# Spilled expert blocks of 64 rows in two tiles instead of 96 in three, in an encoder-layer kernel

## The chip, the cores and the metric

One core of a Trainium2 chip. The metric is the device time of one execution in microseconds (us); of several runs the median is given. Engines are called PE (matmul), DVE, ACT, POOL (vector, activation and general engine) and SP (which only issues loads and stores here).

## The reference, cut to what matters

One layer of a streaming encoder for 1024 prompt rows and 32 sample rows: two recurrent/attention mixers, cross attention to a memory, and a mixture of experts (MoE) with 32 experts of 1024 x 512. A layer norm follows each. The change touches the MoE alone:

```
lg = xt @ w_group + b_group;  g_sel = argmax(lg)              # one of 4 groups
le = (xt @ w_expert + b_expert).reshape(T, 4, 8)
top_v, top_i = top_k(le[rows, g_sel], 2)                      # two experts of 8 in the group
gate = softmax(top_v) * softmax(lg)[rows, g_sel]
for each row and each of its two experts e:
    h = silu(x @ w_gate[e]) * (x @ w_up[e])
    y[row] += gate * (h @ w_down[e])
x = layer_norm(alpha * x + y)
```

There are 1056 rows, so 2112 pairs of row and expert, 66 for an expert in the mean.

## The kernel before

All work is in float32. Projections, attention and recurrence fill the first 1200 us. Then routing, the expert stage and the last norm follow.

*Routing* (DVE from line 1827 on). Masks of the chosen experts are summed over rows, so that each pair gets its rank within its expert (`RR`) and each expert its count (`cnt`). An expert has one dense block of C = 96 rows. What goes beyond is put into spilled blocks of the same size: `ovn` is the number of them for each expert, `TB_` for each pair the block of its expert that it falls into (0 is the dense one), and `RR` becomes its row in that block. There are `NOVER` = 22 places for spilled blocks and `NB` = 54 blocks in all. PE multiplies one-hot matrices `pick` (rows of a block, written by DVE and POOL) and `place` (blocks, two halves of NB columns: the token and its gate) into `tables` (L838), spreads them over the partitions (L845), and DVE turns them into the gather indices `tok_idx` and the gates (L1896 to L1900). `over3` (L1885) finds for each spilled block its expert; `over_i` has the experts and, as its last entry, the number of spilled blocks in use, `n_over`.

*Dense experts*, 32 in a row, double-buffered: POOL gathers the expert's rows from `x2_dram` in three gathers, one for each tile of 32 rows (L2131); DVE transposes them; PE makes gate and up (L864, 192 matmuls of 32 x 256 columns), ACT and DVE the silu and the transposed h, PE the down product (L873, 96 matmuls), ACT scales by the gate, POOL scatters to `y_dram` (L2121). SP's queue loads three weight matrices of 2 MB an expert, gate and up after the gate/up of the expert two before, down after its down product.

*Spilled blocks* (`spilled` on every engine). They run behind the dense experts, under conditions on `n_over`: two written out, the others in a loop. Their weights go through the same two buffers (`sp` L1140 to L1146; the first two blocks wait for the last dense experts). PE does gate/up tile by tile into a bank of its own for each tile (L920), then down tile by tile as the h of each tile arrives (L932); the silu of a tile runs as soon as its gate/up is there (ACT L1420, DVE L1972 to L1980). ACT evacuates two tiles after the second down tile and the third after the third, stores the block with four DMAs (`store_y`, L1379) and waits for them to land before it goes on. On POOL the blocks are not a loop: `NOVER` conditions stand one after another, each with the gathers of one block (L2150 to L2155).

*The end.* When all is stored, ACT raises `fin_ready` (L1446), POOL gathers for every row its two results from `y_dram` (L2166), PE adds them (L954), and the last norm and the stores follow.

`y_dram` has NB x 96 rows of 4 KB and is filled with zeros early (ACT L1196, one DMA). DVE and ACT wait for that DMA (`zeros_out`, L1524 and L1219) before the first attention scores, as the zeros' place is used there.

Of the kernel before, what the change touches and what calls it, by code (L numbers as in the profile page):

```python
# [8 lines left out]
ALU = mybir.AluOpType  # L9
ACT = mybir.ActivationFunctionType  # L10
# [4 lines left out]
KD = D // P  # L15
SEQ, DEC = 1024, 32
T = SEQ + DEC
NT = (T + P - 1) // P
# [4 lines left out]
G, EG = 4, 8  # L23
NE = G * EG
# [1 line left out]
KE = DE // P  # L26
C = 96
NS = C // 32
NOVER = (2 * T) // C
NB = NE + NOVER  # L30
ALPHA = 2.0 ** 0.25
LN_EPS, RMS_EPS = 1e-5, 1e-6
# [19 lines left out]
def build(nc, io):  # L52
    ctx = ExitStack()
    with ctx:
# [64 lines left out]
        def view(_at, names, **n):  # L119
            size = 1  # L120
            for v in n.values():
                size *= v
            return at(_at, size).rearrange(f"p ({names}) -> p {names}", **n)
# [72 lines left out]
        def route(names, **n):  # L196
            size = 1
            for v in n.values():
                size *= v
            rt[0] += size  # L200
            return view(rt[0] - size, names, **n)
# [17 lines left out]
        assert rt[0] <= R + 23552  # L219
        rt[0] = R + 19968  # L220
        overs = route("i e", i=4, e=NE)
        over3 = route("j e", j=NOVER, e=NE)
        gates = route("n a", n=NB, a=NS)
        tokq = route("n a", n=NB, a=NS)
        none_q = route("n a", n=NB, a=NS)
# [208 lines left out]
        def _(pe):  # L434
# [476 lines left out]
            def spilled(j, b, turn_n):  # L911
                pe.wait_ge(o_xt, j + 1)
                pe.wait_ge(o_w[b], 32 * turn_n + 32)
                if isinstance(j, int):
                    pe.wait_ge(y_ready, NE - 1 + j)
                for a in range(NS):
                    for k in range(KD):
                        for q in range(4):
                            out = psum[32 * q:32 * q + 32, (3 * b + a) * BANK:(3 * b + a) * BANK + 256]
                            last = mm(out.rearrange("p (m n) -> p m n", m=2), xeT[:, b, a, k, :],  # L920
                                      gu[b][:, :, k, q * P:(q + 1) * P], start=(k == 0), stop=(k == KD - 1))
                    last.then_inc(o_gu, 1)
                pe.wait_ge(o_down[b], 16 * turn_n + 16)
                if isinstance(j, int) and j == 0:
                    pe.wait_ge(y_ready, NE)
                else:
                    pe.wait_ge(o_y, j)
                for a in range(NS):
                    pe.wait_ge(o_h, 3 * j + a + 1)
                    for k in range(KE):  # L930
                        for q in range(4):
                            last = mm(O_Y[32 * q:32 * q + 32, a * 256:(a + 1) * 256], hhT[:, b, a, k, :],  # L932
                                      wd[b][:, k, q * 256:(q + 1) * 256], start=(k == 0), stop=(k == KE - 1))
                    if a > 0:
                        last.then_inc(o_dn, 1)

            with pe.If(n_over > 0):
                spilled(0, 0, 0)
# [21 lines left out]
        def _(sp):  # L960
# [173 lines left out]
            def spilled(j, b):  # L1134
                e = sp.value_load(over_i[0:1, bass.ds(j, 1)], min_val=0, max_val=NE - 1)
                if isinstance(j, int):
                    sp.wait_ge(gu_done, NE - 1 + j)
                else:
                    sp.wait_ge(o_gu, 3 * j - 3)
                sp.dma_start(gu[b][:, 0], dyn(gate_w, e)).then_inc(o_w[b], 16)  # L1140
                sp.dma_start(gu[b][:, 1], dyn(up_w, e)).then_inc(o_w[b], 16)
                if isinstance(j, int):
                    sp.wait_ge(y_done, NE - 1 + j)
                else:
                    sp.wait_ge(o_dn, 2 * j - 2)
                sp.dma_start(wd[b], dyn(down_w, e)).then_inc(o_down[b], 16)  # L1146
# [26 lines left out]
        def _(act):  # L1173
# [200 lines left out]
            gate_rows = [psum[:, a * BANK:a * BANK + NS * 256].rearrange("p (s m n) -> p s m n", m=2, n=P)[:, :, 0, :]  # L1374
                         for a in (0, 2)]

            def store_y(rows, slot, s):
                for q in range(4):
                    act.dma_start(rows[:, 256 * q:256 * q + 256].rearrange("(a t) n -> t a n", t=32),  # L1379
                                  ye[slot][32 * q:32 * q + 32]).then_inc(s, 16)  # L1380

            def y_rows(e, b, slot, turn_n):

                act.wait_ge(y_done, e + 1)
# [28 lines left out]
            def spilled(j, b):  # L1413
                if isinstance(j, int) and j == 0:
                    act.wait_ge(h_ready, NE)
                else:
                    act.wait_ge(o_h, 3 * j)
                for a in range(NS):
                    act.wait_ge(o_gu, 3 * j + a + 1)
                    A(sg[:, a, :], psum[:, (3 * b + a) * BANK:(3 * b + a) * BANK + P], ACT.Exp, scale=-1.0)\  # L1420
                        .then_inc(g_exp, 1)
                act.wait_ge(o_gate, j + 1)
                act.wait_ge(o_dn, 2 * j + 1)
                if isinstance(j, int):
                    act.wait_ge(y_out[b], 16 * NS * NE // 4)
                for a in range(2):
                    A(ye[b][:, a, :], O_Y[:, a * 256:(a + 1) * 256], ACT.Copy, scale=gate2[:, b, a:a + 1])
                act.wait_ge(o_dn, 2 * j + 2)
                A(ye[b][:, 2, :], O_Y[:, 512:768], ACT.Copy, scale=gate2[:, b, 2:3]).then_inc(o_y, 1)
                act.wait_ge(o_y, j + 1)  # L1430
                store_y(y_dram[bass.ds(j * C + NE * C, C), :], b, o_out)
                act.wait_ge(o_out, 64 * j + 64)
                A(lnv[:, 0:1], eps_ln, ACT.Copy)

# [27 lines left out]
        def _(dve):  # L1462
# [381 lines left out]
            dve.wait_ge(evac["dve"], jobs[("RK",)][3] + 1)  # L1844
            cnt, ovn, oend, ost = (overs[:, i, :] for i in range(4))

            link(TS(ovn, cnt, 1.0 / C, -(C / 2 + 0.5) / C, ALU.mult, ALU.add))
            link(TS(ovn, ovn, ROUND, -ROUND, ALU.add, ALU.add))
            link(TS(ovn, ovn, 0.0, None, ALU.max))
            link(V.tensor_tensor_scan(oend, one_col.to_broadcast([P, NE]), ovn, 0.0, ALU.mult, ALU.add))  # L1850
# [2 lines left out]
            link(V.tensor_reduce(RR, products, AX.X, ALU.add))  # L1853
            of_chosen(ost, OO)

            link(TS(TB_, RR, 1.0 / C, -(C / 2 - 0.5) / C, ALU.mult, ALU.add))
            link(TS(TB_, TB_, ROUND, -ROUND, ALU.add, ALU.add))
            STT(RR, TB_, -float(C), RR, ALU.mult, ALU.add).then_inc(places_ready, 1)
            link(TS(TA, TB_, 1.0, None, ALU.is_ge))
            link(TT(OO, OO, TB_, ALU.add))  # L1860
            link(STT(OO, OO, float(NE - 1), EE, ALU.add, ALU.subtract))
# [60 lines left out]
            def turn_x(b):  # L1922
                return V.transpose(xeT[:, b], xe[:, b].rearrange("p s (d k) -> p s k d", k=KD))  # L1923
# [32 lines left out]
            n_over = dve.value_load(over_i[0:1, NOVER:NOVER + 1], min_val=0, max_val=NOVER)  # L1956

            def spilled(j, b, turn_n):
                dve.wait_ge(o_x[b], 16 * NS * turn_n + 16 * NS)
                turn_x(b).then_inc(o_xt, 1)  # L1960
                if isinstance(j, int):
                    dve.wait_ge(y_ready, NE - 1 + j)
                    dve.wait_ge(y_done, NE - 1 + j)
                else:
                    dve.wait_ge(o_y, j - 1)
                    dve.wait_ge(o_dn, 2 * j - 2)
                V.tensor_copy(gate2[:, b:b + 1, :], gates[:, bass.ds(j + NE, 1), :]).then_inc(o_gate, 1)
                for a in range(NS):
                    n, s_a = 12 * j + 4 * NE + 4 * a, sg[:, a, :]
                    gate, up = (psum[:, (3 * b + a) * BANK + m * P:(3 * b + a) * BANK + m * P + P] for m in range(2))  # L1970
                    dve.wait_ge(g_exp, 3 * j + NE + a + 1)
                    TS(s_a, s_a, 1.0, None, ALU.add).then_inc(silu_step, 1)  # L1972
                    dve.wait_ge(silu_step, n + 1)
                    V.reciprocal(s_a, s_a).then_inc(silu_step, 1)
                    dve.wait_ge(silu_step, n + 2)
                    TT(s_a, s_a, gate, ALU.mult).then_inc(silu_step, 1)
                    dve.wait_ge(silu_step, n + 3)
                    TT(hh[:, a, :], s_a, up, ALU.mult).then_inc(silu_step, 1)
                    dve.wait_ge(silu_step, n + 4)
                    V.transpose(hhT[:, b, a], hh[:, a, :].rearrange("p (d k) -> p k d", k=KE)).then_inc(o_h, 1)  # L1980
# [42 lines left out]
        def _(pool):  # L2023
# [101 lines left out]

            x2_quarters = x2_dram.rearrange("t (q n) -> (t q) n", q=4)

            def gather(e, b, done):

                for a in range(NS):  # L2130
                    pool.indirect_dma_start(out=xe[:, b, a, :], out_offset=None, in_=x2_quarters,  # L2131
                                            in_offset=bass.IndirectOffsetOnAxis(ap=tok_idx[:, e, a:a + 1], axis=0),
                                            bounds_check=4 * T - 1, oob_is_err=False)\
                        .then_inc(done[a], 16)
# [13 lines left out]
            for j in range(NOVER):  # L2148
                if j == 2:
                    for e in range(NE - 3, NE):  # L2150
                        scatter(e)
                with pool.If(n_over > j):
                    if j < 2:
                        pool.wait_ge(xt_ready, NE - 1 + j)
                    else:  # L2155
                        pool.wait_ge(o_xt, j - 1)
                    gather(NE + j, j % 2, [o_x[j % 2]] * NS)
                if j < 2:
                    scatter(NE - 5 + j)

# [39 lines left out]
```

## Time and profile before

| | us |
|---|---|
| median of three timed runs | 1838.14 (1835.23 to 1840.77) |
| the profiled execution | 1831.85 |
| its span, first to last instruction | 1830.1 |
| PE busy | 1732.0 |
| two spilled blocks on PE | 1742.4 to 1773.5 |

The profile is one execution. Its span is what the engines' instructions cover; the execution's own time has 1.75 us more around it. Times in the rows below are from the span's start. "Busy" of PE is not PE at its peak: matmul ends are modelled. The chain of waits is followed back from the last instruction, at each step to what released it. A row of it gives its start, its length, the engine and line that it lies on, and how many instructions are merged.

### The profile page before, as it was taken

The page shows a single profiled execution, that of the slowest core. Times are in us where ns is not written, and L with a number is a line of the kernel's source. Part 1 is how long each engine was busy: PE and PEld are TensorE (multiplying, and loading weights), DVE is VectorE, ACT ScalarE, POOL GpSimd, SP SyncE. Part 2 cuts the span into 40 slices and gives each one's busy share as a digit, 9 for nine tenths or more (in the row PEclk, how much of TensorE's full clock was granted, in tenths as well). Part 3 has the DMA queues.
Part 4 walks back from the last instruction along what each step waited for, and adds up shares of the span by engine and source line. Part 5 has one row for each costly group of instructions (what it writes and reads, how often), then busy time and mean ns, then how long its engine had stood idle before and what let it go on. Part 6 is the DMA issues. An engine that isn't in the chain of part 4 may idle for free. (4 is left out here: it accounts for less than half of the span.)

```text
span 1830.1 us, 34543 instructions
## 1 busy us (share of the span) xinstructions
PE 1732.0 (95%) x15263; PEld 1085.3 (59%) x15263; DVE 746.0 (41%) x1174; ACT 326.1 (18%) x741; POOL 293.5 (16%) x291
## 2 busy tenths in 40 slices
PE   8999999999999999999998999849999999999976
PEld 4565556645666644445666665536666666666642
DVE  1213456514766753310104333564434443344337
ACT  1212224401334210110002111000111110111116
POOL 2100000001322000000000000043333333333223
PEclk9999999999999999999999999769999999999997
DMA  8951011001002041253100000549999999999957
GB/s 276 310 187 47 1 45 51 1 1 49 1 5 98 5 161 35 73 195 115 46 26 32 24 23 12 192 156 391 420 422 421 422 420 421 422 422 416 391 219 276
DMA packets 66230, 330.70 MB, mean 181 GB/s; under 512 B 14948, under 2 KB 17352, under 8 KB 53088
## 3 DMA queue, kind: packets, MB, share of 16 engines
q1 hardware_dynamic: 47856, 280.70, 38.5%
q0 software_dynamic: 12192, 26.76, 4.0%
q10 hardware_dynamic: 6096, 22.02, 3.9%
q8 instruction: 63, 1.03, 0.2%
q14 instruction: 23, 0.19, 0.0%
HBM read 288.05 MB, written 50.23 MB: 185 GB/s over the span
## 5 line engine op out<-in xcount | busy, mean ns | idle before, releaser
L864 PE MATMUL psum<-arena 128*32 128x256 f32 x6144 | 339.8, 381 | 20.1 <-issue 13.3
L864 PEld LDWEIGHTS psum<-arena 128*32 128x32 f32 x6144 | 230.6, 111 | 127.9 <-issue 33.1
L461 PE MATMUL psum<-arena 128*128 128x512 f32 x640 | 282.2, 600 | 2.9 <-issue 2.9
L1468 DVE COPY arena<-psum 128x512 f32<-128x512 f32 (+6 forms) x128 | 83.8, 663 | 368.0 <-PE psum L461 201.2
L461 PEld LDWEIGHTS psum<-arena 128*128 128x128 f32 x640 | 121.9, 193 | 149.9 <-issue 149.5
L684 PE MATMUL psum<-arena 128*128 128x352 f32 x576 | 177.9, 460 | 0.0
L873 PE MATMUL psum<-arena 128*32 128x256 f32 x3072 | 172.3, 379 | 0.5 <-DVE arena L1920 0.5
L446 PE MATMUL psum<-arena 128*128 128x352 f32 x576 | 170.8, 460 | 0.1
L1178 ACT ACTIVATE arena<-psum 128x128 f32<-128x128 f32 (+7 forms) x193 | 94.1, 497 | 344.8 <-PE psum L439 243.8
L2131 POOL DMA_INDIRECT arena<-x_rows,consts x102 | 103.8, 1017 | 282.8 <-DVE arena L1923 254.0
L873 PEld LDWEIGHTS psum<-arena 128*32 128x32 f32 x3072 | 116.3, 110 | 50.1 <-DVE arena L1920 1.0
L446 PEld LDWEIGHTS psum<-arena 128*128 128x128 f32 x576 | 109.6, 190 | 61.1 <-issue 0.8
L684 PEld LDWEIGHTS psum<-arena 128*128 128x128 f32 x576 | 106.7, 191 | 52.7 <-issue 0.2
L1910 DVE TENSOR_SCALAR arena<-arena 128x384 f32<-128x384 f32 x32 | 11.5, 360 | 298.2 <-ACT arena L1396 298.2
L439 PEld LDWEIGHTS psum<-consts,arena 128*128 128x128 f32 (+4 forms) x783 | 91.0, 153 | 53.8 <-issue 35.3
L439 PE MATMUL psum<-consts,arena 128*128 128x128 f32 (+4 forms) x783 | 113.1, 276 | 10.3 <-POOL consts L2040 4.7
L719 PE MATMUL psum<-arena 128*128 128x512 f32 x256 | 111.3, 593 | 0.0
L2121 POOL DMA_INDIRECT y_blocks<-arena,consts x96 | 96.0, 1000 | 51.2 <-issue 28.4
L1706 DVE SCALAR_TENSOR_TENSOR arena<-arena,psum 128x1024 f32<-128x1024 f32 x16 | 19.5, 1221 | 161.0 <-PE psum L461 88.2
L719 PEld LDWEIGHTS psum<-arena 128*128 128x128 f32 x256 | 48.2, 190 | 57.9 <-issue 57.7
L1912 DVE RECIPROCAL arena<-arena 128x384 f32<-128x384 f32 x32 | 81.7, 2553 | 1.1
L2065 POOL TENSOR_TENSOR arena<-arena 128x1024 f32<-128x1024 f32 x4 | 8.2, 2039 | 432.9 <-DVE arena L1590 432.9
(279 smaller groups left out, 1653.0 us busy)
## 6 DMA issues: line engine op xcount, KB each, us to landing
arena<-in_moe_w_down SPq DMA_DIRECT2D x34, 2048.0 KB, 21.4
arena<-in_moe_w_gate SPq DMA_DIRECT2D x34, 2048.0 KB, 14.5
arena<-in_moe_w_up SPq DMA_DIRECT2D x34, 2048.0 KB, 21.1
y_blocks<-arena ACTq DMA_DIRECT2D x1, 20736.0 KB, 102.2
arena<-in_w_in SPq DMA_DIRECT2D x6, 2048.0 KB, 9.8
arena<-in_x_prompt SPq DMA_DIRECT2D x9, 512.0 KB, 3.3
arena<-in_w_out SPq DMA_DIRECT2D x2, 2048.0 KB, 8.1
arena<-in_xa_wk SPq DMA_DIRECT2D x2, 2048.0 KB, 11.9
```

What stands on the lines that cost most here:

```text
L439: return nc.tensor.transpose(out, a, ident[0:n, 0:n])
L446: last = mm(ps[:, c * BANK:c * BANK + THIRD], lhs(k), rhs[:, k, c * THIRD:(c + 1) * THIRD], start=(k == 0), stop=(k == KD - 1))
L461: last = mm(ps[0:n, c * 512:(c + 1) * 512], lhs(k), rhs(k)[:, c * 512:(c + 1) * 512], start=(k == 0), stop=(k == KD - 1))
L684: last = mm(psum[:, bank * BANK:bank * BANK + THIRD], w_z[name][:, k, m * P:(m + 1) * P], xT[:, k, third(c)], start=(k == 0), stop=(k == K ...
L719: last = mm(psum[0:n, b:b + BANK], mixT[:, k, cols_of(t)], wrows[:, k, c * 512:(c + 1) * 512], start=(k == 4), stop=(k == 3))
L864: last = mm(out, xeT[:, b, a, k, :], gu[b][:, :, k, j * P:(j + 1) * P], start=(k == 0), stop=(k == KD - 1))
L873: last = mm(B_Y[b][32 * j:32 * j + 32, a * 256:(a + 1) * 256], hhT[:, b, a, k, :], wd[b][:, k, j * 256:(j + 1) * 256], start=(k == 0), sto ...
L1178: take(A(out, src, ACT.Copy), key)
L1468: take(V.tensor_copy(out, src), key)
L1912: V.reciprocal(sg, sg).then_inc(silu_step, 1)
L2121: pool.indirect_dma_start(out=y_quarters, out_offset=bass.IndirectOffsetOnAxis(ap=y_idx[:, e, a:a + 1], axis=0), in_=ye[e % 4][:, a, :], i ...
L2131: pool.indirect_dma_start(out=xe[:, b, a, :], out_offset=None, in_=x2_quarters, in_offset=bass.IndirectOffsetOnAxis(ap=tok_idx[:, e, a:a + ...
```

## The change

A spilled block now holds `OVER_ROWS` = 64 rows, in the tiles 1 and 2 of the three; tile 0 of it is left out on every engine. An expert's first 96 rows stay dense; what goes beyond is counted in blocks of 64, and a row's place in its block starts at 32. There are 32 places for spilled blocks instead of 22, and 64 table columns a half instead of 54. `y_dram` grows with NB (each block keeps 96 rows in it). `over3` gets a place of its own in memory. The semaphore counts follow (two a block instead of three).

```diff
-NOVER = (2 * T) // C
+OVER_ROWS = C - 32
+NOVER = 32
 NB = NE + NOVER
@@ pe, spilled
-                for a in range(NS):
+                for a in (1, 2):
                     for k in range(KD):              # gate and up of tile a
...
-                for a in range(NS):
-                    pe.wait_ge(o_h, 3 * j + a + 1)
+                for a in (1, 2):
+                    pe.wait_ge(o_h, 2 * j + a)
...
-                    if a > 0:
-                        last.then_inc(o_dn, 1)
+                    last.then_inc(o_dn, 1)
@@ act, spilled
-                for a in range(2):
-                    A(ye[b][:, a, :], O_Y[:, a * 256:(a + 1) * 256], ACT.Copy, scale=gate2[:, b, a:a + 1])
+                A(ye[b][:, 1, :], O_Y[:, 256:512], ACT.Copy, scale=gate2[:, b, 1:2])
                 act.wait_ge(o_dn, 2 * j + 2)
                 A(ye[b][:, 2, :], O_Y[:, 512:768], ACT.Copy, scale=gate2[:, b, 2:3]).then_inc(o_y, 1)
                 act.wait_ge(o_y, j + 1)
-                store_y(y_dram[bass.ds(j * C + NE * C, C), :], b, o_out)
+                rows = y_dram[bass.ds(j * C + NE * C + 32, OVER_ROWS), :]
+                for q in range(4):
+                    act.dma_start(rows[:, 256 * q:256 * q + 256].rearrange("(a t) n -> t a n", t=32),
+                                  ye[b][32 * q:32 * q + 32, 1:3]).then_inc(o_out, 16)
@@ dve, routing
-            link(TS(ovn, cnt, 1.0 / C, -(C / 2 + 0.5) / C, ALU.mult, ALU.add))
+            link(TS(ovn, cnt, 1.0 / OVER_ROWS, 0.5 - (C + 0.5) / OVER_ROWS, ALU.mult, ALU.add))
...
-            link(TS(TB_, RR, 1.0 / C, -(C / 2 - 0.5) / C, ALU.mult, ALU.add))
+            link(TS(TB_, RR, 32.0, 1.0 / OVER_ROWS, ALU.max, ALU.mult))
+            link(TS(TB_, TB_, 0.5 / OVER_ROWS - 1.0, None, ALU.add))
             link(TS(TB_, TB_, ROUND, -ROUND, ALU.add, ALU.add))
-            STT(RR, TB_, -float(C), RR, ALU.mult, ALU.add).then_inc(places_ready, 1)
+            STT(RR, TB_, -float(OVER_ROWS), RR, ALU.mult, ALU.add).then_inc(places_ready, 1)
@@ dve, spilled
-                dve.wait_ge(o_x[b], 16 * NS * turn_n + 16 * NS)
-                turn_x(b).then_inc(o_xt, 1)
+                dve.wait_ge(o_x[b], 32 * turn_n + 32)
+                V.transpose(xeT[:, b, 1:3], xe[:, b, 1:3].rearrange("p s (d k) -> p s k d", k=KD)).then_inc(o_xt, 1)
...
-                for a in range(NS):
+                for a in (1, 2):                     # silu of tile a
@@ pool
-                    gather(NE + j, j % 2, [o_x[j % 2]] * NS)
+                    gather(NE + j, j % 2, [o_x[j % 2]] * NS, (1, 2))
```

## Rows read from the trace of the kernel before

**Rows 1.** The page: span, and PE's busy time, its share and instructions.
```profile
span 1830.1 us, 34543 instructions
PE 1732.0 (95%) x15263; PEld 1085.3 (59%) x15263; DVE 746.0 (41%) x1174; ACT 326.1 (18%) x741; POOL 293.5 (16%) x291
```

**Rows 2.** The page's DMA issues: what, queue, count, KB each, us to landing.
```profile
arena<-in_moe_w_gate SPq DMA_DIRECT2D x34, 2048.0 KB, 14.5
y_blocks<-arena ACTq DMA_DIRECT2D x1, 20736.0 KB, 102.2
```

**Rows 3.** The chain of waits in the spilled blocks: start, us, what, instructions.
```profile
1742.40 10.36 PE psum L920 x192
1752.76 5.18 PE psum L932 x96
1757.94 10.36 PE psum L920 x192
1768.30 5.22 PE psum L932 x96
```

**Rows 4.** SP's instructions in order of time: start, us, queue, line, what.
```profile
1736.58 0.33 SPq L1146 DMA_DIRECT2D arena<-in_moe_w_down  x1
...
1738.19 0.48 SPq L1141 DMA_DIRECT2D arena<-in_moe_w_up  x1
1742.46 0.33 SPq L1146 DMA_DIRECT2D arena<-in_moe_w_down  x1
```

**Rows 5.** DMA issues of 1736.5-1736.7, 1738.0-1738.3 and 1742.3-1742.6, last column us to landing.
```profile
arena<-in_moe_w_down SPq DMA_DIRECT2D x1, 2048.0 KB, 10.7
...
arena<-in_moe_w_up SPq DMA_DIRECT2D x1, 2048.0 KB, 19.3
...
arena<-in_moe_w_down SPq DMA_DIRECT2D x1, 2048.0 KB, 20.0
```

**Rows 6.** Busy by stretch: us, PE, PEld, DVE, ACT, POOL, granted clock, DMA share, GB/s.
```profile
1736.00:1759.00 23.00, 22.51 (x420) 13.41 (x415) 10.99 (x22) 4.55 (x12) 5.90 (x6) 1.00 1.00 403
```

**Rows 7.** DVE in order of time: the last transpose of block 1's third tile.
```profile
1770.60 0.42 DVE L1980 STREAM_TRANSPOSE arena<-arena 128x128 f32<-128x128 f32 x1
```

**Rows 8.** Busy by stretch as in rows 6, around two pauses of PE before the routing.
```profile
1143.00:1144.00 1.00, 0.00 (x0) 0.00 (x0) 1.00 (x2) 0.12 (x1) 0.00 (x0) 1.00 0.14 53
...
1146.00:1147.00 1.00, 1.00 (x7) 0.93 (x7) 0.90 (x5) 0.00 (x0) 0.00 (x0) 0.50 0.85 328
...
1183.00:1184.00 1.00, 0.62 (x3) 0.62 (x4) 0.96 (x2) 0.33 (x1) 0.00 (x0) 0.58 1.03 442
```

**Rows 9.** The chain of waits: gate/up of the first two dense experts.
```profile
1223.40 22.94 PE psum L864 x384
```

**Rows 10.** DVE in order of time, in the routing: start, us, line, operation, shapes.
```profile
1205.62 0.18 DVE L1857 TENSOR_SCALAR arena<-arena 128x18 f32<-128x18 f32 x1
...
1207.13 0.61 DVE L1875 TENSOR_TENSOR arena<-arena 128x432 f32<-128x432 f32 x1
...
1213.59 0.89 DVE L1885 TENSOR_TENSOR arena<-arena 128x704 f32<-128x704 f32 x1
```

**Rows 11.** In order of time: the zero store's issue, and the first attention steps.
```profile
36.38 0.39 ACTq L1196 DMA_DIRECT2D y_blocks<-arena  x1
...
154.14 0.30 DVE L1532 TENSOR_TENSOR psum<-psum,consts 128x128 f32<-128x128 f32 x1 [0.74 <-PE psum L564]
...
154.89 0.37 ACT L1238 ACTIVATE arena<-psum,consts 128x128 f32<-128x128 f32 x1 [7.15 <-DVE consts L1533]
...
159.45 0.27 PE L439 MATMUL psum<-consts,arena 128*128 128x128 f32 x1
```

**Rows 12.** In order of time: ACT behind block 1, POOL's next step; idle before in brackets.
```profile
1779.02 0.20 ACT L1433 ACTIVATE consts<-consts 128x1 f32<-128x1 f32 x1 [5.00 <-DMA y_blocks<-arena]
1779.34 0.20 ACT L1446 ACTIVATE consts<-consts 128x1 f32<-128x1 f32 x1
1779.82 0.90 POOL L2166 DMA_INDIRECT arena<-y_blocks,consts  x1 [31.79 <-ACT consts L1446]
```

More of the change, by code:

```diff
@@ L221, in build @@
         overs = route("i e", i=4, e=NE)
-        over3 = route("j e", j=NOVER, e=NE)
+        over3 = view(R + 21504 + 2 * NT * G, "j e", j=NOVER, e=NE)
         gates = route("n a", n=NB, a=NS)
@@ L1138, in spilled @@
                 else:
-                    sp.wait_ge(o_gu, 3 * j - 3)
+                    sp.wait_ge(o_gu, 2 * j - 2)
                 sp.dma_start(gu[b][:, 0], dyn(gate_w, e)).then_inc(o_w[b], 16)
@@ L1375, in _ @@
                          for a in (0, 2)]
[L1377 to L1380, printed above, removed]
             def y_rows(e, b, slot, turn_n):
@@ L1416, in spilled @@
                 else:
-                    act.wait_ge(o_h, 3 * j)
-                for a in range(NS):
-                    act.wait_ge(o_gu, 3 * j + a + 1)
+                    act.wait_ge(o_h, 2 * j)
+                for a in (1, 2):
+                    act.wait_ge(o_gu, 2 * j + a)
                     A(sg[:, a, :], psum[:, (3 * b + a) * BANK:(3 * b + a) * BANK + P], ACT.Exp, scale=-1.0)\
@@ L1967, in spilled @@
                 V.tensor_copy(gate2[:, b:b + 1, :], gates[:, bass.ds(j + NE, 1), :]).then_inc(o_gate, 1)
-                for a in range(NS):
-                    n, s_a = 12 * j + 4 * NE + 4 * a, sg[:, a, :]
+                for a in (1, 2):
+                    n, s_a = 8 * j + 4 * NE + 4 * (a - 1), sg[:, a, :]
                     gate, up = (psum[:, (3 * b + a) * BANK + m * P:(3 * b + a) * BANK + m * P + P] for m in range(2))
-                    dve.wait_ge(g_exp, 3 * j + NE + a + 1)
+                    dve.wait_ge(g_exp, 2 * j + NE + a)
                     TS(s_a, s_a, 1.0, None, ALU.add).then_inc(silu_step, 1)
@@ L2126, in _, with gather @@
             x2_quarters = x2_dram.rearrange("t (q n) -> (t q) n", q=4)
-            def gather(e, b, done):
-                for a in range(NS):
+            def gather(e, b, done, tiles=range(NS)):
+                for a in tiles:
                     pool.indirect_dma_start(out=xe[:, b, a, :], out_offset=None, in_=x2_quarters,
```

## The prediction

> **What bounds the kernel now.** I read the page first (span, engine shares), then the chain of waits from its end backwards, then around the two spilled blocks the issues of the load queue with their landing times, the busy times by stretch, and last the engines' order of time in the routing. TensorE (PE) is busy for 95% of 1830.1 us [rows 1], so work taken from it counts, if nothing else is late there. 34 gate loads are issued [rows 2]: 32 experts and two spilled blocks. The chain shows these two at the end of the MoE stage, all on PE and without a gap: gate/up of block 0 from 1742.40, down from 1752.76, gate/up of block 1 from 1757.94, down from 1768.30 to 1773.52 [rows 3]. Each gate/up is 10.36 us for three tiles (3.45 a tile), each down 5.18 (1.73 a tile). The reader should see that "on PE" isn't "because of PE" there: the DMA engines are at a share of 1.00 from 1736 to 1759 at 403 GB/s [rows 6], and the up weights of block 1, issued at 1738.19, take 19.3 us [rows 4, 5], so they land at 1757.5, 0.45 us before PE takes them up.
>
> **How many blocks.** The reference's routing of these inputs gives two experts more than 96 rows: 158 and 105; the next has 94. Over 96 they have 62 and 9 rows, so both forms need one block each: two before, two after.
>
> **The change, part by part** (times on the clock of before). *Block 0.* One tile less: 3.45 + 1.73 = 5.18 us of PE. But the third tile was also a cover. From the end of a gate/up tile to its turned h there are 2.72 us (1768.30 [rows 3] to 1770.60 + 0.42 [rows 7]), for exp, four DVE steps and a transpose. With three tiles PE had two tiles of down (3.46) to do meanwhile; with two it has one (1.73) and waits about 1.05 with the hand-over. So gate/up ends at 1749.3, h of the last tile at 1752.0, down at 1753.8: 4.1 us earlier than 1757.94. Its down weights are there (1736.58 + 10.7 = 1747.3 [rows 4, 5]).
> *Block 1.* Its up weights land at 1757.5 as before: the load's issue waits for the last dense experts, not for block 0, and the queue ahead of it is the same. Block 0's store now goes out at about 1754.4 and shares the DMA engines with that load: 0.26 MB at 403 GB/s [rows 6] is 0.6 us at most; I take half. So block 1 starts at about 1757.9, where it started before, and block 0's 4.1 us are lost in a wait for weights. What remains is block 1's own saving, the same 4.1 us. Its down weights (1742.46 + 20.0 = 1762.5 [rows 4, 5]) are still ahead of their use at 1764.8.
> *The clock.* PE, so far without a pause, now stands for 1.05 us and then for 4.1 us. The trace has like pauses: it was idle through 1143 to 1144 at clock 1.00, and at 1146 to 1147, busy again, it had 0.50; after a pause to 1183.4 the clock is 0.58 in 1183 to 1184 [rows 8]. That is the fall from 2.4 to 1.2 GHz. Its price stands in the chain: two gate/up of 192 matmuls after a pause took 22.94 us [rows 9] where two at full clock take 20.72 [rows 3], so 2.2 us. Bounds: 0 (no fall) and 6.9 (all of block 1's gate/up at half speed). I take 2.2. The Trainium skill speaks against the change at this place: "TensorE: Matmul & The Clock Gate", section "HAM oscillation — how this bites in real kernels", says that a burst of matmuls shorter than the wait for its next transfer lets the clock drop, so that the next burst starts at half rate. By that rule the sum below is as it stands; without it it would be 2.2 us lower; the trace agrees in its pauses before the routing and shows nothing of it among the experts, where no such pause exists.
> *The last store and what follows.* PE's end to ACT's next step is 5.5 us (1773.52 [rows 3] to 1779.02 [rows 12]): evacuation, four issues, landing. A third fewer bytes: between 0 and 1.8 (a third of 5.5); I take 0.5, as issue and latency stay. The gather of the pairs and the last norm shift as a whole.
> *Routing.* Here nothing but routing runs, and DVE is its chain, so every step counts. One more scalar step: 0.2 [rows 10]. The tables get 64 columns a half for 54. An operation on 432 elements takes 0.61 us and one on 704 takes 0.89 [rows 10], 1.03 ns an element. Six large place operations of 80 more elements: 0.5. The block-to-expert compare and its sum, 704 to 1024 elements: 2 x 0.33 = 0.66. The transposes' PE work and four reads of the tables: some 0.25. Sum 1.6, at 1.2 to 2.0; PE's own table matmuls grow beside it and end first. The first weight loads of the expert stage wait for the first expert, so the whole stage moves by 1.6.
> *Zero fill.* y_dram grows from 54 to 64 x 96 rows. The store, issued at 36.38 [rows 11], lands after 102.2 us [rows 2], at 138.6; in proportion to its bytes it would take 121 and land at 157.5. DVE's first step that waits for it ran at 154.14, the exponential after it at 154.89 for 0.37, and PE wants its result no earlier than 159.45 [rows 11]; so the fill may land up to 158.3 and cost nothing. I take 0; what if it is later stands below.
> *POOL.* Ten more skipped conditions; 6 gathers of the blocks become 4. POOL waits 31.79 us after its last scatter [rows 12], with 20 such conditions in that time, so 30 are hidden at any price below 0.98 us. ACT passes a skipped condition and four waits in 0.12 us (1779.22 to 1779.34 [rows 12]). I take 0. The smaller transposes, the dropped copy on ACT and the other index offsets lie beside PE or loads: 0.
>
> **Sum.** +1.6 (routing) − 4.1 (block 1) + 2.2 (clock) − 0.5 (store) = −0.8. The span goes from 1830.1 to 1829.3, that execution from 1831.85 to 1831.0. It was quicker than all three timed runs (1835.23 to 1840.77); I take the difference over to their median: 1838.14 − 0.8 = 1837.3. The bounds of the terms alone give −4.7 to +4.8.
>
> **Rivals.** *The clock holds.* For: the fall comes late, not yet at 1143 to 1144, and could fall behind block 1's gate/up. Against: both pauses of [rows 8] were followed by it. −3.0: 1835.1.
> *The weights come in time*, because a freer DMA queue brings block 1's up weights by 1753.8. For: only 0.45 us show that they are late at all. Against: the share of 1.00 [rows 6]. Both blocks save 4.1 without a fall: 1.6 − 8.2 − 0.5 = −7.1: 1831.0.
> *The zero fill is late.* It decides from 158.3 on. If the next 2 MB weight load (L1002, after the queries' projection) falls into its end and is served first, the fill loses 5.2 us more (2.1 MB at 403 GB/s [rows 6]) and lands at 162.7: 4.4 us on the first attention scores: 1841.7. Against: that load is one of two that take turns.
> *POOL's conditions set the end* (the other side). At the bound, 31.79 / 20 = 1.59 us each, 30 take 47.7 and the pair gathers begin at 1797.3 instead of 1778.9, so +17.6: 1855.7. It decides from 0.98 us on. Against: ACT's 0.12.
> *The change doesn't keep the count*: an expert with more than 160 rows needs two blocks of 64. The largest has 158, two rows of room. A third block's loads queue behind the others: its up weights would land 2 x 5.1 us (2.1 MB at 403 GB/s) after 1762.5, at 1772.7; PE then ends at 1784, 10.6 later than before, with clock and routing +13: 1851.
>
> **How the numbers follow.** Forecast 0.60; the clock holds 0.18; weights in time 0.08; zero fill late 0.05; POOL 0.04; a third block 0.03; something else 0.02. A measurement of this kernel tells about 0.3% (5.5 us) from no change. Below 1832.6 lie the weights in time and a little scatter of the two likeliest: 0.12. Above 1843.7 lie POOL, the third block, the worst of the zero fill and scatter: 0.10. Between: 0.78. The range takes in the weights in time and most of the late fill and leaves out POOL and the third block: 1831 to 1842.5.
>
> **What would show it.** In the profile of after: gate/up of the blocks with 128 matmuls each and down with 64; a PE pause of about 4 us ended by a DMA before block 1, whose up weights land near 1757.5 + 1.6; a granted clock of 0.5 in part of block 1's gate/up; one wait of about 1 us within each down; the first expert 1.6 us later; two blocks (34 gate loads); the zero store landing before PE's first wait in attention. If block 1 starts 4 us earlier, or the clock stays, the tail steps are wrong; if the first expert isn't later, the routing step is; if POOL's pair gathers begin after ACT's last step by more than 0.5 us, POOL's is.

## The result, and the profile after

| | before | after |
|---|---|---|
| time, median of 20 runs each | 1837.65 us (1831.43 to 1847.25) | 1842.4 us (1836.69 to 1853.84) |
| ratio | | 1.0036, 95% interval 1.0019 to 1.0052 |
| profiled execution, its span | 1831.85, 1830.1 us | 1842.33, 1840.6 us |
| granted clock, mean | 0.976 | 0.971 |

In the text, before and after name the two kernels. The change makes the kernel a little slower: 4.75 us between the medians, where 0.8 us less was forecast. The time lies within the range given; the sign is that of the rival "the zero fill is late". Executions of one kernel lie up to 17 us apart; in every profile but that of before PE runs a part of attention (mostly within 217 to 250 us) at half clock, and the longer this stretch, the longer the execution (6 to 7 us of it in h2's, which took 1833.55 us, some 30 in f2's of 1848.05); so the kernels are compared by medians and intervals, and the profiles stretch by stretch.

The page of after, to be held against [rows 1, 2]: span, TensorE, and the two DMA issues (KB each, us to landing).

```profile
span 1840.6 us, 34152 instructions
PE 1732.7 (94%) x15071; PEld 1084.1 (59%) x15071; DVE 742.7 (40%) x1165; ACT 324.9 (18%) x737; POOL 294.1 (16%) x289
arena<-in_moe_w_gate SPq DMA_DIRECT2D x34, 2048.0 KB, 15.9
y_blocks<-arena ACTq DMA_DIRECT2D x1, 24576.0 KB, 125.8
```

PE has 192 instructions fewer and is busy as long as before: what its two tiles less saved was lost at a lower clock (the mean is 0.971 for 0.976). And it stands still for longer. 34 gate loads: two spilled blocks, as said. The zero fill takes 125.8 us where 102.2 stood in [rows 2].

**First place: the first attention scores.** After, in order of time, the steps that stood in [rows 11], with the idle time and its releaser in brackets:

```profile
157.69 1.88 PE L549 MATMUL psum<-arena 128*128 128x512 f32 x4
...
162.26 0.30 DVE L1529 TENSOR_TENSOR psum<-psum,consts 128x128 f32<-128x128 f32 x1 [8.90 <-DMA y_blocks<-arena]
163.00 0.37 ACT L1238 ACTIVATE arena<-psum,consts 128x128 f32<-128x128 f32 x1 [15.31 <-DVE consts L1530]
163.52 0.48 PE L440 MATMUL psum<-consts,arena 128*128 128x128 f32 x1 [3.95 <-ACT arena L1238]
...
164.21 3.62 PE L549 MATMUL psum<-arena 128*128 128x512 f32 x4
```

The steps are those of before in the same order, and now what starts them is the landing of the fill (36.4 + 125.8 = 162.2). PE's first product of exp is at 163.52 instead of 159.45, 4.07 later. And the next four matmuls take 3.62 us where four like them took 1.88 ahead of the pause: the clock has fallen. The stretches of after say so (columns as in rows 6 of before; the granted clock is the third number from the right):

```profile
158.00:163.00 5.00, 1.57 (x4) 0.38 (x2) 0.70 (x3) 0.00 (x0) 0.00 (x0) 0.96 0.07 27
163.00:164.00 1.00, 0.48 (x3) 0.49 (x3) 0.89 (x4) 0.92 (x4) 0.00 (x0) 0.50 0.10 35
168.00:169.00 1.00, 0.86 (x11) 0.55 (x13) 0.97 (x3) 0.00 (x0) 0.00 (x0) 0.50 0.00 0
229.00:230.00 1.00, 1.00 (x2) 0.58 (x3) 0.29 (x1) 0.07 (x1) 0.00 (x0) 0.50 0.00 0
```

By 175 us PE is 6.5 us behind, 2.4 of it from the half clock. A second half-clock stretch (227 to 234, PE busy throughout) adds 2.75, and small steps from 750 us on add 0.8. The routing's first step (PE's rank matmuls) is at 1207.22 instead of 1197.18: 10.04 later.

**Second place: the routing.** From that step to the first expert after takes 29.00 us (1207.22 to 1236.22) where before took 26.22: 2.78 more, 1.6 forecast. PE's table matmuls, the stretch of after and then DVE's step behind them:

```profile
1221.40:1228.60 7.20, 7.09 (x36) 6.91 (x36) 5.74 (x13) 0.00 (x0) 2.46 (x3) 0.58 0.01 2
...
1228.66 0.29 DVE L1890 COPY consts<-psum 96x128 f32<-96x128 f32 x1 [1.18 <-PE psum L839]
```

and the same stretch of before:

```profile
1210.90:1216.00 5.10, 4.96 (x36) 4.81 (x36) 4.76 (x13) 0.00 (x0) 2.19 (x3) 0.71 0.01 3
```

The 36 matmuls have 128 columns for 108, and the clock is 0.58 for 0.71: 7.09 us for 4.96. DVE, which was the chain, now waits 1.18 us for PE. Before already had next to no room there: the table matmuls ended at 1215.91, and the step of DVE that takes them up began at 1216.05.

```profile
1210.95 4.96 PE L838 MATMUL psum<-arena 128*96 128x108 f32 x36 [11.37 <-DVE arena L1879]
...
1216.05 0.27 DVE L1892 COPY consts<-psum 96x108 f32<-96x108 f32 x1
```

**Third place: the spilled blocks**, where the gain is. The chain of waits of after, for [rows 3], and the issue and the landing of block 1's up weights:

```profile
1755.93 6.95 PE psum L921 x128
...
1765.56 1.93 PE psum L933 x32
1767.49 3.04 issue
1770.53 8.66 PE psum L921 x128
...
1781.88 1.98 PE psum L933 x32
```

```profile
1751.72 0.48 SPq L1141 DMA_DIRECT2D arena<-in_moe_w_up  x1
...
arena<-in_moe_w_up SPq DMA_DIRECT2D x1, 2048.0 KB, 18.7
```

Block 0 runs from 1755.93 to 1767.49, 11.56 us (15.54 before). Then PE stands for 3.04 us until the up weights are there (1751.72 + 18.7 = 1770.4). Block 1's gate/up takes 8.66 us where block 0's takes 6.95: the stretch 1771 to 1772 has a granted clock of 0.50. From the start of the last dense down to PE's end before took 36.5 us (1737.01 to 1773.52), after 33.3 (1750.54 to 1783.86): 3.2 gained.

**The sum of the two profiles**: 10.04 until the routing, 2.78 in it, 0.71 among the experts, −3.2 in the blocks, 0.3 behind them: 10.67 at the gather of the pairs (1779.82 to 1790.49), and the span is 10.5 longer. The medians differ by 4.75 only: before's profiled execution has no half-clock stretch between 217 and 250 and is one of its quickest (1831.85, where its runs begin at 1831.43); after's has one and lies at its median. So the 10.67 is the difference of these two executions and not the price of the change.

### The profile page after: what moved, and what is told of

Its sections match the earlier page's. It is cut to its first block and busy times, and to the rows that moved or that the text cites. A ratio compares the mean times of both kernels' runs of the same rounds, so it can differ in the third digit from the quotient of the medians.

```text
span 1840.6 us, 34152 instructions
## 1 busy us (share of the span) xinstructions
PE 1732.7 (94%) x15071; PEld 1084.1 (59%) x15071; DVE 742.7 (40%) x1165; ACT 324.9 (18%) x737; POOL 294.1 (16%) x289
## 5 line engine op out<-in xcount | busy, mean ns | idle before, releaser
L440 PEld LDWEIGHTS psum<-consts,arena 128*128 128x128 f32 (+4 forms) x783 | 91.7, 154 | 59.6 <-issue 36.5
## 6 DMA issues: line engine op xcount, KB each, us to landing
y_blocks<-arena ACTq DMA_DIRECT2D x1, 24576.0 KB, 125.8
```

What stands on the lines that cost most here:

```text
L440: return nc.tensor.transpose(out, a, ident[0:n, 0:n])
```

## Experiments

Each is timed beside the kernel before on the same chip; the ratio is to that. "Tail" is from the start of the last dense down to PE's end, 36.5 before and 33.3 after.

**e1: the two-tile blocks with 22 columns.** After, so that the fill and the routing's widths are those of before:

```diff
-NOVER = 32
+NOVER = 22
```

> The changed kernel with 22 places for spilled blocks instead of 32, so that the tables (54 columns) and the zero fill (54 x 96 rows) are those of before; the two blocks have two tiles of 32 rows each. Theory 'the fill' (the larger zero fill ends after attention wants to begin, and the clock falls in the pause): attention starts as before and only the tail's gain is left, 2 to 4 us faster than before, ratio 0.998 to 0.999. Rival 'the blocks' (the tile change itself costs): as slow as the changed kernel, ratio 1.003 or more.

1834.49 us, 0.9981 (0.9961 to 1.0002). The fill takes 101.9 us and PE has no pause before its first product of exp; routing 26.41; tail 33.1 (1749.16 to 1782.26). The blocks alone are a gain of 3.4 us in the tail, which the time shows at the edge of its interval.

**e2: the larger tables alone.** Before, three tiles:

```diff
-NOVER = (2 * T) // C
+NOVER = 32
```

> The kernel before with 32 places for spilled blocks, so tables of 64 columns and a zero fill of 64 x 96 rows, blocks still of 96 rows in three tiles. Theory 'the fill': 162 us instead of 139 for the fill's landing, first expert 10 to 13 us later than before, nothing won at the end, ratio 1.005 to 1.007. Rival 'the blocks': ratio 1.000 to 1.001.

1842.11 us, 1.0024 (1.0002 to 1.0047), below the 1.005 to 1.007 expected. The fill takes 125.8 us, the values of attention are stored (SP) at 276.42 (267.56 before, 276.80 after), the routing takes 27.74, the tail 37.0. So the loss lies in the sizes.

**e5: the larger buffer alone.** Before; `y_dram` has 64 x 96 rows, all filled, the tables as they were:

```diff
-        y_dram = nc.dram_tensor("y_blocks", [NB * C, D], F32, kind="Internal").ap()
+        y_dram = nc.dram_tensor("y_blocks", [64 * C, D], F32, kind="Internal").ap()
-                                  zeros[0:C, :].unsqueeze(1).to_broadcast([C, NB, D])).then_inc(zeros_out, 16)
+                                  zeros[0:C, :].unsqueeze(1).to_broadcast([C, 64, D])).then_inc(zeros_out, 16)
```

> The kernel before with a block store of 64 x 96 rows, all filled with zeros (25.2 MB instead of 21.2); nothing else is changed, tables have 54 columns. Theory 'the fill': the fill lands near 162, PE pauses about 4 us before the first attention scores, the granted clock is 0.5 for some us after it, ratio 1.004 to 1.006. Rival 'the tables': ratio 1.000.

1841.23 us, 1.0016 (0.9992 to 1.004): below the 1.004 to 1.006 expected, and by its interval not to be told from no change. Its profile has the places of e2: the fill 125.5 us, the values stored at 276.19, the routing 26.29 as before. So the larger tables add nothing to the shift up to the routing; the 1.5 us that e2 has more lie in the routing. Not all of the shift is shown to be the buffer's, though: e2 and e5 too have the second half-clock stretch (227 to 234), and f1 below stores its values at 275.84 with no late fill, after 20 us at half clock.

**f1: the same fill from 128 partitions.** After; 24576 KB as before it, spread otherwise:

```diff
-                    act.dma_start(y_dram.rearrange("(j p) n -> p j n", p=C),
-                                  zeros[0:C, :].unsqueeze(1).to_broadcast([C, NB, D])).then_inc(zeros_out, 16)
+                    act.dma_start(y_dram.rearrange("(j p) n -> p j n", p=P),
+                                  zeros.unsqueeze(1).to_broadcast([P, NB * C // P, D])).then_inc(zeros_out, 16)
```

> The changed kernel with its zero fill written from 128 partitions (48 x 4 KB each) instead of 96 (64 x 4 KB each): the same 6144 rows and bytes. Theory 'shape' (the fill is late because few DMA engines end late, not because of its bytes; 20.5 MB from 128 partitions landed after 56 us in an earlier run, 20.7 MB from 96 after 102): it lands after some 68 us, near 105, attention starts as before, 5 to 6 us faster than the changed kernel, ratio to before 0.998 to 1.000. Rival 'bytes': it lands past 154 and the ratio stays at 1.003.

```profile
y_blocks<-arena ACTq DMA_DIRECT2D x1, 24576.0 KB, 71.3
```

1838.71 us, 0.9981 (0.996 to 1.0002). The bytes alone don't set the fill's time: the same 24576 KB take 71.3 us for 125.8. Routing 28.96 with the table matmuls at 7.04, so the routing's extra is apart from the fill. Block 1's gate/up took 7.11 here after a pause of 2.95: the clock did not fall.

**e3: blocks packed, 64 rows each.** After with `y_dram` of 5120 rows (20480 KB), filled from 128 partitions, and two more DVE steps in the routing for the places:

```diff
+Y_ROWS = NE * C + NOVER * OVER_ROWS
...
+            link(STT(OO, EE, -float(NE - 1), TA, ALU.add, ALU.mult))
+            link(STT(TB_, OO, -32.0, TB_, ALU.mult, ALU.add))
```

> The changed kernel with 64 rows for a spilled block in the block store instead of 96: 5120 rows are allocated and filled with zeros (before: 5184, changed: 6144); the tables keep 64 columns, and two short steps on DVE are added for the rows' places. Theory 'the fill': the fill lands near 139 again and attention starts as before; routing is 1.6 to 3 us later, the tail 3 us earlier: ratio 0.999 to 1.001. Rival 'the tables' (the loss comes from the 64 columns): ratio 1.003 as the changed kernel.

1835.9 us, 0.9994 (0.9968 to 1.002); the fill 56.4 us, table matmuls 7.12, block 1's gate/up 8.51 to 8.55. No loss, no gain that can be told.

**h1: only the weight load moved behind the fill.** After; what is asked is why the fill took 125.8 us, when its bytes in proportion to [rows 2] give 121.1. The load went out at 145.59 and PE needs its weights only behind the value store at 276.8:

```diff
+            sp.wait_ge(zeros_out, 16)
             load("zi")
```

> The kernel after, but SP waits for the zero fill's landing before it issues the 2 MB weight load that went out at 145.59 (PE uses that weight only after the value store at 276.8, so the later load should cost nothing). Theory A, the load takes the place of the fill's last packets: the fill lands after 24576 / 20736 x 102.2 = 121.1 us instead of 125.8, at 157.5; that is ahead of 158.3, so PE's pause of 3.95 us before its first product of exp falls to under 0.5, the half clock after it goes too, and the time goes from 1842.4 to 1835 to 1838, a ratio of 0.996 to 0.999. Theory B, the fill grows more than its bytes by itself: it still lands after 125 to 126 us, the pause stays between 3.5 and 4.5 and the ratio between 1.002 and 1.005.

```profile
y_blocks<-arena ACTq DMA_DIRECT2D x1, 24576.0 KB, 121.6
...
157.56 0.62 SPq L1002 DMA_DIRECT2D arena<-in_w_in  x1
...
159.02 0.27 PE L440 MATMUL psum<-consts,arena 128*128 128x128 f32 x1
```

1838.03 us, 0.9996 (0.9974 to 1.0018). The fill takes 4.2 us less, and that is enough: PE's pause of 3.95 us is gone, and so is the half clock behind it. Held against before matmul by matmul, PE is 0.43 us ahead from 100 to 218 us, without a step; after is 6.5 us behind from 164 on. (What h1's value store has more than before's, 272.84 for 267.56, comes in a half-clock stretch from 219 to 233.) The interval just misses that of after (1.0019 to 1.0052). One wait on one load gives back what after had lost. How little of the DMA engines the fill used by then, in h1 (the last two numbers are their share and GB/s):

```profile
130.00:140.00 10.00, 10.00 (x36) 6.40 (x35) 0.00 (x0) 2.09 (x2) 0.00 (x0) 1.00 0.40 99
140.00:150.00 10.00, 10.00 (x30) 5.49 (x29) 0.00 (x0) 2.09 (x2) 0.00 (x0) 1.00 0.20 47
150.00:157.00 7.00, 6.53 (x26) 3.23 (x25) 0.90 (x3) 0.00 (x0) 0.00 (x0) 1.00 0.07 26
```

and in f1, from 128 partitions:

```profile
60.00:100.00 40.00, 39.67 (x276) 24.30 (x275) 14.46 (x29) 9.52 (x18) 7.14 (x1) 1.00 1.02 404
```

From 96 partitions the fill ends with ever fewer of the 16 DMA engines at work (0.20 x 16 is about three, 0.07 x 16 about one), at 47 and 26 GB/s, where f1 has 404. The trace keeps sixteen landings for such a transfer: those of h1's fill come between 103.7 and 157.5 us (five by 105.5, ten by 132.0, the last three at 148.7, 151.7 and 157.5), those of f1's between 105.0 and 107.0.

The 2 MB load that after issues into this end meets the late ones. It takes 19.4 us there and 8.0 in before:

```profile
arena<-in_w_in SPq DMA_DIRECT2D x1, 2048.0 KB, 19.4
```

```profile
arena<-in_w_in SPq DMA_DIRECT2D x1, 2048.0 KB, 8.0
```

Of its sixteen landings in after thirteen come by 153.7 and three at 155.7, 158.9 and 165.0 (in before all between 153.2 and 153.6). From 153.6 on, when one landing of the fill is outstanding, the fill moves 3.8 of its packets a us in after and 5.9 in h1. Load and fill slow each other down at the fill's late end.

**f4 and g1: before with a fill from 128 partitions.** Is the quicker fill worth something to before? Its 5184 rows aren't a multiple of 128; f4 issues two DMAs (40 x 128 rows, then 64), g1 has 5248 rows and one:

```diff
...
+                    act.dma_start(y_dram[0:40 * P, :].rearrange("(j p) n -> p j n", p=P),
+                                  zeros.unsqueeze(1).to_broadcast([P, 40, D])).then_inc(zeros_out, 16)
+                    act.dma_start(y_dram[40 * P:NB * C, :], zeros[0:NB * C - 40 * P, :]).then_inc(zeros_out, 16)
```

> The kernel before with its zero fill from 128 partitions (40 x 4 KB each) and a second small one for the last 64 rows. Theory: the fill ended 15.5 us early anyway, so nothing changes, ratio 0.999 to 1.001. Rival: the quicker fill takes DMA time from the first loads or frees it for the others, ratio beyond 0.998 or 1.002.

> The kernel before with a block store of 5248 rows, filled with zeros by one DMA from 128 partitions (41 x 4 KB each). Theory 'shape': the fill lands near 95 instead of 139, nobody waited for it, so the time is that of the kernel before, ratio 0.999 to 1.001; the 35 us of the form with two fill DMAs were the second issue, which held ACT for 39.8 us. Rival 'contention' (a quick fill harms the loads beside it): ratio 1.01 or more.

g1: 1843.8 us, 1.0008 (0.9982 to 1.0034), the fill 58.3 us: nothing, as before's fill was in time anyway. f4: 1874.82 us, 1.0166 (1.0139 to 1.0193), for a reason of its own, seen in its order of time and in one of its stretches:

```profile
36.57 39.82 ACTq L1198 DMA_DIRECT2D y_blocks<-arena  x1
76.44 1.56 ACT L1178 ACTIVATE arena<-psum 128x512 f32<-128x512 f32 x3 [39.72 <-issue]
...
45.00:77.00 32.00, 0.00 (x0) 0.00 (x0) 0.00 (x0) 0.56 (x2) 0.00 (x0) 0.57 1.02 410
```

The second issue, behind 20480 KB on the same queue, held ACT for 39.8 us, and PE did nothing from 45 to 77. g1, with one issue, has no such hold.

**f2, f3, g3: the pauses of the blocks**, all on top of f1. f2 fills PE's two pauses in block 0 with matmuls whose results nobody reads (16 and 52):

```diff
+                    if isinstance(j, int) and j == 0:
+                        for i in range((16, 52)[a - 1]):
+                            mm(psum[32 * (i % 4):32 * (i % 4) + 32, 0:256], ident[:, 0:32], consts[:, 0:256], start=True, stop=True)
```

> As the run with the fill from 128 partitions, and PE runs matmuls whose result nobody reads in its two pauses around the end of block 0's down (16 behind its first tile, 52 behind its second). Theory 'clock' (block 1's gate/up runs at half clock because of the pause): the granted clock stays 1.00 there, that gate/up takes 6.9 us instead of 8.7, PE's end is 1.5 to 2 us earlier against block 1's start. Rival 'something else slows block 1' (transfers, the store): still 8.5 us or more.

1838.74 us, 0.9988 (0.997 to 1.0006). Block 1's gate/up took 7.09 at a clock of 1.00; as f1 itself has 7.11 there, this run alone doesn't show that the added matmuls kept the clock. The 52 took 5.79 us, longer than the pause that they were to fill: block 1 began 22.9 us behind the start of the last dense down (19.9 in f1), and the tail is 34.6 for f1's 32.7.

f3 issues block 0's gate and up loads ahead of the last dense down load (and no longer where they stood):

```diff
+            with sp.If(n_over > 0):
+                e0 = sp.value_load(over_i[0:1, 0:1], min_val=0, max_val=NE - 1)
+                sp.wait_ge(gu_done, NE - 1)
+                sp.dma_start(gu[0][:, 0], dyn(gate_w, e0)).then_inc(o_w[0], 16)
+                sp.dma_start(gu[0][:, 1], dyn(up_w, e0)).then_inc(o_w[0], 16)
+            load_down(NE - 1, 1, NE - 2)
```

> As the run with the fill from 128 partitions, and SP issues block 0's gate and up loads ahead of the last dense expert's down load, so that the DMA engines don't run low before them. Theory 'weights' (block 1 waits for its up weights, which follow in one stream): the stream is 3 to 4 us ahead, block 1's gate/up begins 1 us or less behind block 0's down instead of 3.0, and the tail is 2 to 4 us shorter. Rival 'block 1 waits for something else' (its rows, bank or the store): the pause of 3.0 us stays.

```profile
1756.20 8.04 PE L874 MATMUL psum<-arena 128*32 128x256 f32 x96 [4.31 <-issue]
...
1773.88 1.94 PE L933 MATMUL psum<-arena 128*32 128x256 f32 x32 [1.00 <-DVE arena L1983]
1775.63 7.09 PE L921 MATMUL psum<-arena 128*32 128x256 f32 x128
```

1843.38 us, 1.0001 (0.9979 to 1.0022). The pause ahead of block 1 is gone (1773.88, and 1775.63 next), and one of 4.31 us stands before the last dense down, whose weights now come later, with 8.04 us for it instead of 5.39. The wait only moves, as the DMA engines have no room to give (share 1.01 at 423 GB/s from 1756.2 to 1764): this order doesn't bring in block 0's 4 us.

g3 lets ACT go into block 1 without waiting for block 0's store. After showed that wait, which the prediction had not:

```profile
1776.33 0.20 ACT L1430 ACTIVATE consts<-consts 128x1 f32<-128x1 f32 x1 [8.30 <-DMA y_blocks<-arena]
```

```diff
-                act.wait_ge(o_out, 64 * j + 64)
-                A(lnv[:, 0:1], eps_ln, ACT.Copy)
+                if not isinstance(j, int) or j > 0:
+                    act.wait_ge(o_out, 64 * j + 64)
+                    A(lnv[:, 0:1], eps_ln, ACT.Copy)
...
```

> The changed kernel with the fill from 128 partitions; ACT no longer waits for block 0's store to land before block 1's exponentials (it waits for both stores at the end). Theory 'store wait' (with two tiles, that store goes out while loads fill the DMA engines, lands 8.2 us later and holds block 1's first exponential): that exponential follows its gate/up tile at once, PE's wait before block 1's first down tile (0.1 to 1.6 us in the runs so far) is gone, the tail up to 1.6 us shorter. Rival: no change of the tail.

1838.34 us, 0.9995 (0.9976 to 1.0015). The exp of block 1 now follows its tile (1771.41), and the tail is 33.2. In f1 and h1, where block 1's gate/up ran at full clock, the wait did hold up its down by 1.64 and 1.77 us; where the clock had fallen it lay beneath the slow matmuls (0 to 0.23 us of it were left in after, e1 and e3). One hides the other: with the clock fallen, taking the store's wait away shows nothing.

**g2: PE kept at work ahead of the table matmuls**, on f1: 40 matmuls that nobody reads:

```diff
+            pe.wait_ge(places_ready, 1)
+            for i in range(40):
+                mm(psum[32 * (i % 4):32 * (i % 4) + 32, 3 * BANK:3 * BANK + 256], ident[:, 0:32], consts[:, 0:256], start=True, stop=True)
```

> The changed kernel with the fill from 128 partitions, and PE runs 40 matmuls whose result nobody reads ahead of the table matmuls, from the time on at which DVE has the places. Theory 'routing at half clock' (the table matmuls took 7.1 us instead of 5.6 because the clock was 0.5 throughout): they take 5.6 us or less, the first expert begins 27 to 28 us after the rank matmuls instead of 29.0. Rival 'columns alone': 7 us as before.

```profile
1221.68 4.17 PE L842 MATMUL psum<-arena 128*96 128x128 f32 x36
```

1841.98 us, 0.9985 (0.9965 to 1.0005). The table matmuls take 4.17 us for f1's 7.04, and the routing (rank matmuls to first expert) 27.95 for 28.96: what it has over the forecast is, but for 0.1, PE's clock.

**g4 and h2: the gains together.** g4 is e3 with g2's and g3's edits; h2 is e1 with g3's.

> The changed kernel with 64 rows a block in the store (5120 rows, filled from 128 partitions), the matmuls ahead of the tables, and ACT's store wait at the end. Theory: attention starts as before, routing 1.2 to 1.6 us later than before, the tail 3 to 4.5 us shorter: 2 to 3 us faster than before, ratio 0.998 to 0.999. Rival 'the clock in attention decides' (spells at half clock there differ from execution to execution by some 10 us): the ratio lies within 0.996 to 1.002 whatever the edits.

> The two edits that gained something in the runs so far, together: the two-tile blocks with 22 columns (so the fill is 20736 KB again and lands near 138.3, the routing takes 26.4) and ACT not waiting for block 0's store before block 1. If the gains add up, last dense down to PE's end takes 31.5 to 32.5 us (36.5 before, 33.1 with the tiles alone), and the time is 0.996 to 0.998 of before. Rival: the store's wait was hidden behind block 1's gate/up, then 33.1 stays and the ratio is that of the tiles alone, 0.998. The half-clock stretches in attention, in both kernels, will blur either by several us.

g4: 1842.62 us, 0.9993 (0.9973 to 1.0013). h2: 1836.58 us, 0.9991 (0.9968 to 1.0015); its tail took 34.6, as block 1's gate/up, after a pause of 2.95, took 10.01 us. The gains don't add up, and no version here is faster than before by more than its interval; the nearest are e1 and f1, 0.998.

**What stays open** is the half clock in attention with PE busy, in both kernels. It needs no late fill; e1 has none, and its stretch is:

```profile
220.00:240.00 20.00, 20.00 (x98) 12.79 (x97) 9.64 (x22) 5.42 (x16) 0.00 (x0) 0.50 0.00 1
```

The stretch begins at 218 to 222 us in the kernels without a late fill, at 227 in the three with one (after, e2, e5), where attention is some 6 us later, and at 254 in f4, where it is 34 us later: at about the same place of the program each time. So the 2.75 us of after's second stretch aren't shown to be the fill's. What starts these stretches was not found.

## Why the prediction was wrong, point by point

**Zero fill, taken at 0: the step that failed.** It put the landing at 157.5 in proportion to the bytes, with 0.8 us of room to 158.3. The proportion is right (121.6 us measured in h1, for 121). The step failed on the load at 145.59: the 2 MB went into the fill's end, and it landed at 162.2. The rival "the zero fill is late" had that collision with its landing (162.7 priced) and its wait (4.4 priced, 4.07 measured), and a chance of 0.05; "that load is one of two that take turns" was the argument against, but it goes out at 145.63 in before and at 145.59 in after. Two things in it were otherwise: the load was not served first but slowed too (19.4 us for 8.0), and the half clock behind PE's pause, 2.4 us, was left out. Without the load, h1 has 1838.03 where 1837.3 was forecast; that this is so near is in part luck, as h1's routing has the 1.2 us too many below, and in its profile the clock of block 1's gate/up didn't fall (7.11 us).

What could have been read: the trace of before already had the fill's long end, with a DMA share far below 1.00 while it was still out (its sixteen landings come between 90.3 and 138.6). The stretch of before:

```profile
130.00:140.00 10.00, 10.00 (x35) 6.46 (x34) 0.00 (x0) 2.09 (x2) 0.00 (x0) 1.00 0.10 34
```

A few engines were late, and the next load was due at 145.6, ahead of the landing forecast for 157.5.

**Routing, 1.6: too small by 1.2.** The DVE terms stand: in e2, where DVE does not wait for PE (its table matmuls took 5.56), the routing took 27.74 − 26.22 = 1.5 more. What failed is "PE's own table matmuls grow beside it and end first": before had 0.14 us of room for that, at the lower clock they became the chain (1.18 us of waiting), and g2 takes that away.

**Block 0, nothing kept: right, but for 0.9.** It was 3.98 us shorter (4.1 forecast), and PE then waited for block 1's up weights, 3.04 us. Block 1 began 0.9 earlier against the last dense down, as those weights took 18.7 us for 19.3 and had had 0.45 to spare.

**Block 1, −4.1, and the clock, +2.2: right.** Its gate/up, down and their pause took 13.33 us for 15.58, 2.25 saved where 1.9 was forecast; the clock cost 1.71. The wait of about 1 us within the down is there (1.00 in most kernels). The price of the clock isn't one number: over the nine kernels with two tiles and the pause, block 1's gate/up took 7.11 (f1 and h1), 8.42 to 8.71 in six of them and 10.01 (h2), after pauses of 2.9 to 3.2 us, within the bounds of 0 to 6.9; so that 2.2 came near the 1.71 of after is in part luck. The Trainium skill, "TensorE: Matmul & The Clock Gate", section "HAM oscillation — how this bites in real kernels", has a burst of matmuls that is shorter than the wait for its next transfer, and the next one starts at half rate. Here block 0's 11.56 us stand ahead of a wait of 3.04, so the prediction took the section beyond its case; a burst after a wait did start at half clock in after (8.66 us for 6.95) and not in f1 (7.11).

**The last store, −0.5: wrong in sign.** From PE's end to ACT's next step it takes 5.83 us in after (1783.86 to 1789.69) for 5.50: a third fewer bytes made it no shorter.

**POOL, 0: right.** POOL still waits 28.94 us for ACT ahead of the pair gather:

```profile
1790.49 0.90 POOL L2164 DMA_INDIRECT arena<-y_blocks,consts  x1 [28.94 <-ACT consts L1443]
```

**The number of blocks: right**, two. (In the rival of a third block the terms come to 14.4 with routing and clock, not 13; it bears on nothing here.)

## What to carry to other kernels

A transfer that is hidden now has a margin, and growing it spends the margin: compare the margin with all else that is due on the DMA engines before the landing, not with the bytes alone. Where the DMA share is far below 1.00 while one large transfer is still out, look whether a few engines carry its end, as here (0.20 and 0.07 in h1), and try another shape (f1) before anything else. And a tile taken from PE's end saves its time only up to the next load, with a pause whose clock is to be priced too.

## What was not expected of the hardware

- A zero fill from 96 partitions took 101.9 to 102.3 us for 20736 KB and 125.5 to 125.8 for 24576 KB (121.6 without the load in its end); from 128 partitions 56.4 us for 20480 KB and 71.3 to 71.4 for 24576 KB. The Trainium skill, "DMA: Bandwidth & Descriptors", section "Rules for kernel authors", asks for 128 partitions for the most bandwidth, and these runs agree; its section "Why a DMA increments its semaphore by 16 and not by 1" counts a tile of 96 partitions among those spread over 16 engines, and the trace agrees with its sixteen landings in h1, which lie up to 53.8 us apart (103.7 to 157.5). Why they end so far apart was not tried.
- A second DMA issued on ACT behind one of 20480 KB held the engine for 39.8 us (f4), where the first issue took 0.45.
- PE ran at half clock for 20 us and more while it was busy without a pause (e1, 220 to 240).
